# Way down of the feed-forward part by seven half-size products in place of eight, on one core of Trainium2

## The reference

```python
        gate, up = jnp.split(rmsnorm(x, g_ffn_pre[l]) @ w_ffn_in[l], 2, axis=-1)
        f = (jax.nn.silu(gate) * up) @ w_ffn_out[l]
        x = x + rmsnorm(f, g_ffn_post[l])
```

## Time and profile before

| | us |
|---|---|
| median of 3 runs | 1862.62 |
| lowest and highest | 1861.3 and 1863.35 |
| profiled execution, its own time | 1862.99 |
| its span, first to last instruction | 1861.2 |
| PE / DVE / ACT busy in the span | 1676.9 / 596.1 / 376.9 |
| mean granted clock of TensorE | 0.939 |

### The profile page before, as it was taken

How to read it: one execution, slowest core, us unless ns; L and a number is a source line. 1 busy time by engine, 2 the same in 40 slices (tenths; PEclk the granted TensorE clock), 3 DMA queues, 4 the chain that set the end, 5 groups by cost and what they waited for, 6 DMA issues and landing times.

```text
span 1861.2 us, 24768 instructions
## 1 busy us (share of the span) xinstructions
PE 1676.9 (90%) x10418; PEld 1070.4 (58%) x10418; DVE 596.1 (32%) x1235; ACT 376.9 (20%) x954; POOL 2.2 (0%) x6
## 2 busy tenths in 40 slices
PE   8999999999999999999999999999997766667666
PEld 5864758884477565688648768898863211102011
DVE  3482127550237422566106474232322000000001
ACT  4252122110224422211102561111202000000001
POOL 0000000000000000000000000000000000000000
PEclk9999999999999999999999999999998778767777
DMA  9313325444442242444453231211479999999997
GB/s 376 120 63 136 133 95 194 149 171 169 181 168 81 91 139 89 173 181 156 174 177 127 96 103 58 70 48 48 163 292 384 421 422 421 422 421 421 422 421 304
DMA packets 54089, 385.22 MB, mean 207 GB/s; under 512 B 6112, under 2 KB 6624, under 8 KB 8032
## 3 DMA queue, kind: packets, MB, share of 16 engines
q1 hardware_dynamic: 52272, 375.15, 51.5%
q10 hardware_dynamic: 1712, 8.52, 1.2%
HBM read 382.60 MB, written 1.05 MB: 206 GB/s over the span
## 4 chain that ended last, share of the span: by engine, by line
PE 70%; DMA 22%; DVE 4%; ACT 2%; issue 1%; SPq 0%; DVEq 0%; ACTq 0%
PE ps L177 50%; DMA arena<-in_stream 16%; DMA ring<-in_stream 5%; PE ps L1744 3%; PE ps L1725 2%; PE ps L1142 2%; PE ps L716 2%; DMA par<-in_stream 1%; PE ps L849 1%; PE ps L181 1%; DVE small L738 1%; PE ps L515 1%; PE ps L1885 1%; DVE arena L734 1%; PE ps L811 1%
## 5 line engine op out<-in xcount | busy, mean ns | idle before, releaser
L177 PE MATMUL ps<-arena 128*128 128x256 f32 (+2 forms) x2070 | 522.2, 550 | 86.3 <-DMA arena<-in_stream 80.8
L177 PEld LDWEIGHTS ps<-arena 128*128 128x128 f32 (+1 forms) x2070 | 271.4, 165 | 302.9 <-DMA arena<-in_stream 176.4
L177 PE MATMUL ps<-ring,arena 128*128 128x512 f32 (+4 forms) x1266 | 413.7, 569 | 33.9 <-DMA ring<-in_stream 29.6
L177 PEld LDWEIGHTS ps<-ring,arena 128*128 128x128 f32 (+1 forms) x1266 | 196.8, 176 | 228.1 <-issue 139.4
L177 PE MATMUL ps<-arena,ring 128*128 128x256 f32 x1260 | 302.2, 388 | 2.1 <-ACT arena L377 2.1
L177 PEld LDWEIGHTS ps<-arena,ring 128*128 128x128 f32 x1260 | 234.1, 191 | 46.9 <-issue 16.2
L2047 PE MATMUL ps<-arena 128*32 128x512 f32 x254 | 170.8, 779 | 0.0
L1097 DVE TENSOR_TENSOR arena<-ps,par 128x512 f32<-128x512 f32 x24 | 16.6, 690 | 263.6 <-ACT arena L1069 263.6
L2185 DVE TENSOR_TENSOR arena<-arena,ps 128x512 f32<-128x512 f32 x8 | 5.5, 687 | 259.4 <-PE ps L2047 259.4
L759 ACT ACTIVATE arena<-arena,small 128x256 f32<-128x256 f32 x112 | 55.7, 498 | 73.7 <-DVE small L746 73.7
L2047 PE MATMUL ps<-ring,arena 128*32 128x512 f32 x90 | 64.4, 823 | 0.0
(11 more groups left out here) (361 smaller groups left out, 1685.0 us busy)
## 6 DMA issues: line engine op xcount, KB each, us to landing
arena<-in_stream SPq DMA_DIRECT2D x175, 1024.0 KB, 26.3
ring<-in_stream SPq DMA_DIRECT2D x160, 1024.0 KB, 5.1
par<-in_stream SPq DMA_DIRECT2D x10, 1024.0 KB, 26.7
const<-in_stream SPq DMA_DIRECT2D x10, 1024.0 KB, 27.0
par<-in_layer_par ACTq DMA_DIRECT2D x3, 1664.0 KB, 8.9
const<-in_const SPq DMA_DIRECT2D x1, 1312.0 KB, 7.4
par<-in_layer_par ACTq DMA_DIRECT2D x2, 516.0 KB, 12.8
x<-in_x ACTq DMA_DIRECT2D x2, 512.0 KB, 7.0
```

The source lines that it names most:

```text
L177: ins = self.pe.e.matmul(out, lhsT, rhs, start=start, stop=stop)
```

## The change

The way down is split in two along each of its three sizes: tokens in blocks 0 and 1, hidden chunks in 0 to 10 ("first") and 11 to 21 ("second"), columns in halves. Each unit now holds chunk j and chunk 11 + j of the weights, as four quarters of 512 columns. Seven products of one block by one half, each with an accumulator of its own over the 11 units, take the place of eight: 1 to 7, on four banks of dve_tiles, two of both_tiles and one of act_tiles (product 1, which is not opened in the ring and waits for ACT's copy of group 9).

DVE makes sums of token blocks for four units at a time (down_tokens, four subtractions or additions up to 128 x 512) and of weights for each unit (down_sums: one subtraction 128 x 1024, which makes two sums, and two of 128 x 512). The sums of units 0 and 10 don't wait for a free buffer; the others wait until the unit two back has been given free. Those for unit 0 stand in the last group of gate and up, the rest behind its hidden rows.

In the last three units products 7 and 4 are left out and follow at the end, all three of 7 and then all three of 4; the three units are given free together behind them. DVE then adds the products to the four output tiles, in SBUF: block 0 from 1, 2, 6, 5 and 3, and its gain and residual; then 7 and block 1. ACT squares the tiles in SBUF, in the order (0,0), (1,0), (1,1), (0,1), and takes the next layer's columns of block 0 behind all four, where it took them ahead of the fourth. DVE takes its own columns of block 0 behind the gains of block 1, ahead of the addition to x.

```diff
+DOWN_ORDER = [(0, 0), (1, 0), (1, 1), (0, 1)]
+DOWN_HELD, DOWN_SUMS = FFN_GROUPS - 3, 4 * (FFN_GROUPS - 1)
...
+    pair = [first_mla + 4096 * i for i in (1, 0)]
+    p.down_both = [p.arena[:, at:at + 1024] for at in (pair[0], pair[1], pair[0] + 2048)]
+    p.down_sums = [[p.arena[:, at + 512 * i:at + 512 * i + 512] for i in range(4)] for at in (pair[0], pair[1], pair[0] + 2048)]
+    p.down_tokens = [[shaped(p.arena[:, at + 512 * i:at + 512 * i + 512], 4, P) for i in range(4)]
+                     for at in (pair[0] + 2048, pair[1] + 2048, first_pr)]
+    p.down_rows = shaped(p.arena[:, pair[1] + 2048:pair[1] + 4096], NB, D)
+    p.down_first, p.down_shared, p.down_middle = [p.arena[:, mark + 512 * i:mark + 512 * i + 512] for i in range(3)]
+    p.down_junk = p.arena[:, first_pr + 2048:first_pr + 3072]
...
+def down_residual_act(p, act, l, raw):
+    act.e.activation(p.small[:, 254:255], p.c("eps"), ACT.Sqrt).then_inc(act.step(), 1)
+    act.e.wait_ge(p.sem("down_first"), l + 1)
+    act.e.activation(p.down_first, p.mark["down_bank"], ACT.Copy).then_inc(
+        act.event("first_copied"), 1)
+    made = [(p.dve_tiles.drained, p.mark["down_dve"] - 3), (p.dve_tiles.drained, p.mark["down_dve"] - 1),
+            (p.both_tiles.drained, p.mark["down_both"] - 1), (p.both_tiles.drained, p.mark["down_both"])]
+    for t, (half, b) in enumerate(DOWN_ORDER):
+        act.e.wait_ge(*made[t])
+        act.e.activation(p.down_junk[:, 512 * (t % 2):512 * (t % 2) + 512], p.down_rows[:, b, half * 512:half * 512 + 512],
+                         ACT.Square, scale=D ** -0.5, accum_out=p.post_squares[:, t:t + 1]).then_inc(act.event("squared"), 1)
+        act.e.wait_ge(p.sem("squared"), 8 + t + 1)
+        base = p.post_squares[:, 4 + b:5 + b]
+        if t % 2 == 0:
+            act.e.activation(base, p.post_squares[:, t:t + 1], ACT.Identity, bias=p.c("eps")).then_inc(act.step(), 1)
+            act.e.wait_ge(act.steps, act.n)
+        else:
+            act.e.activation(p.post_root[:, b:b + 1], p.post_squares[:, t:t + 1], ACT.Sqrt, bias=base).then_inc(
+                act.event("post_root"), 1)
+    block_columns_act(p, act, *raw, 0)
...
+def down_residual_dve(p, dve, gain, raw):
+    first, u2, u4, u3 = p.down_first, p.down_shared, p.down_middle, p.down_first
+    def tile(half, b):
+        return p.down_rows[:, b, half * 512:half * 512 + 512]
+    def summed(out, left, ring):
+        dve.e.wait_ge(ring.full, ring.turn(dve))
+        dve.e.tensor_tensor(out, left, ring.take(dve), ALU.add).then_inc(ring.drained, 1)
+    def gained(half, b):
+        hs = slice(half * 512, half * 512 + 512)
+        dve.e.tensor_tensor(p.hrow[:, b, hs], tile(half, b), gain[:, hs], ALU.mult).then_inc(dve.step(), 1)
+    def added(b):
+        dve.e.wait_ge(dve.steps, dve.n)
+        dve.e.wait_ge(p.sem("post_root"), 4 + b + 1)
+        dve.e.reciprocal(p.rstd[:, b:b + 1], p.post_root[:, b:b + 1]).then_inc(dve.step(), 1)
+        dve.e.wait_ge(dve.steps, dve.n)
+        for half in range(2):
+            hs = slice(half * 512, half * 512 + 512)
+            dve.e.scalar_tensor_tensor(p.x[:, b, hs], p.hrow[:, b, hs], p.rstd[:, b:b + 1], p.x[:, b, hs],
+                                       ALU.mult, ALU.add).then_inc(dve.event("x_ready"), 1)
+    dve.e.wait_ge(p.sem("first_copied"), FFN_GROUPS)
+    summed(tile(0, 0), first, p.dve_tiles)
+    summed(u2, first, p.dve_tiles)
+    dve.e.wait_ge(p.dve_tiles.drained, p.dve_tiles.taken["dve"])
+    fifth = p.both_tiles.banks[p.both_tiles.taken["dve"] % p.both_tiles.size]
+    dve.e.wait_ge(p.both_tiles.full, p.both_tiles.turn(dve))
+    dve.e.tensor_tensor(u4, u2, fifth, ALU.add).then_inc(dve.step(), 1)
+    dve.e.wait_ge(dve.steps, dve.n)
+    summed(tile(1, 0), u4, p.dve_tiles)
+    gained(0, 0)
+    dve.e.wait_ge(p.dve_tiles.drained, p.dve_tiles.taken["dve"])
+    gained(1, 0)
+    added(0)
+    summed(u3, u2, p.dve_tiles)
+    dve.e.wait_ge(p.dve_tiles.drained, p.dve_tiles.taken["dve"])
+    summed(tile(1, 1), u3, p.both_tiles)
+    summed(tile(0, 1), u3, p.both_tiles)
+    dve.e.wait_ge(p.both_tiles.drained, p.both_tiles.taken["dve"])
+    gained(1, 1)
+    gained(0, 1)
+    block_columns_dve(p, dve, *raw, 0)
+    added(1)
...
-    def down(j):
-        u = w.next()
-        pe.e.wait_ge(p.act_tiles.drained, p.mark[f"turned{j}"])
-        for t, (half, b) in enumerate(BY_BLOCK):
-            if j == 0:
-                at = ring.index(acc[t])
-                pe.e.wait_ge(tiles.drained, max(n for n in range(tiles.opened) if n % tiles.size == at) + 1)
-            for c in range(2):
-                f = 2 * j + c
-                last = f == FC - 1
-                o = c * D + half * 512
-                ins = (pe.e.matmul if last else w.mm)(acc[t], p.h1T[:, f, b * P:(b + 1) * P],
-                                                      u[:, o:o + 512], start=f == 0, stop=last)
-                if last:
-                    ins.then_inc(p.dve_tiles.full, 1)
-        w.used()
...
+def down_pe(p, pe, w, tiles, ring, turn):
+    def last_use(bank):
+        at = ring.index(bank)
+        return max(n for n in range(tiles.opened) if n % tiles.size == at) + 1
+    p.mark["last_group"] = tiles.opened
+    acc = {1: p.act_tiles.banks[(p.act_tiles.opened + 1) % p.act_tiles.size]}
+    for name, of in ((2, p.dve_tiles), (6, p.dve_tiles), (3, p.dve_tiles), (7, p.dve_tiles), (5, p.both_tiles), (4, p.both_tiles)):
+        pe.e.wait_ge(of.drained, of.opened - of.size + 1)
+        acc[name] = of.open(pe)
+    p.mark["down_dve"], p.mark["down_both"], p.mark["down_bank"] = p.dve_tiles.opened, p.both_tiles.opened, acc[1]
+    signal = {1: p.sem("down_first"), 2: p.dve_tiles.full, 6: p.dve_tiles.full, 3: p.dve_tiles.full, 7: p.dve_tiles.full,
+              5: p.both_tiles.full, 4: p.both_tiles.full}
+    units = {}
+    def product(j, name):
+        if j == 0 and name == 1:
+            pe.e.wait_ge(p.act_tiles.drained, p.mark[f"turned{FFN_GROUPS - 2}"])
+        if j == 0 and name > 1:
+            pe.e.wait_ge(tiles.drained, last_use(acc[name]))
+        if name == 6:
+            pe.e.wait_ge(p.sem("token_sums"), 4 * (j // 4) + 8)
+            pe.e.wait_ge(p.sem("weight_sums"), DOWN_SUMS + 3 * j + 2)
+        if name == 4:
+            pe.e.wait_ge(p.sem("weight_sums"), DOWN_SUMS + 3 * j + 3)
+        b11, b12, b22, b21 = [units[j][:, 512 * i:512 * i + 512] for i in range(4)]
+        s1, s2, s3, s4 = [both[:, j % 4, :] for both in p.down_tokens[j // 4]]
+        t1, t3, t2, t4 = p.down_sums[down_buffer(j)]
+        first, second = p.h1T[:, j, :], p.h1T[:, FFN_GROUPS + j, :]
+        left, right = {1: (first[:, 0:P], b11), 2: (second[:, 0:P], b21), 3: (s4, b22), 4: (second[:, P:S], t4),
+                       5: (s1, t1), 6: (s2, t2), 7: (s3, t3)}[name]
+        last = j == FFN_GROUPS - 1
+        ins = (pe.e.matmul if last else w.mm)(acc[name], left, right, start=j == 0, stop=last)
+        if last:
+            ins.then_inc(signal[name], 1)
+        return ins
     for j in range(FFN_GROUPS):
-        down(j)
+        units[j] = w.next()
+        if j == FFN_GROUPS - 2:
+            pe.e.wait_ge(p.act_tiles.drained, p.mark[f"turned{FFN_GROUPS - 1}"])
+        for name in (2, 1, 6, 3, 7, 5, 4) if j == 0 else (1, 2, 6, 5, 3) if j >= DOWN_HELD else (1, 2, 6, 5, 3, 7, 4):
+            product(j, name)
+        if j < DOWN_HELD:
+            w.used()
         if j == 1:
             turn(FFN_GROUPS - 1)
+    for name in (7, 4):
+        for j in range(DOWN_HELD, FFN_GROUPS):
+            product(j, name)
+    w.used(FFN_GROUPS - DOWN_HELD)
+def down_buffer(j):
+    return 2 if j == FFN_GROUPS - 1 else j % 2
...
+    def down_tokens(batch):
+        rows = slice(4 * batch, min(4 * batch + 4, FFN_GROUPS))
+        rest = slice(FFN_GROUPS + rows.start, FFN_GROUPS + rows.stop)
+        n = rows.stop - rows.start
+        dve.e.wait_ge(p.act_tiles.drained, p.mark[f"turned{(rest.stop - 1) // 2}"])
+        a11, a21 = p.h1T[:, rows, 0:P], p.h1T[:, rows, P:S]
+        a12, a22 = p.h1T[:, rest, 0:P], p.h1T[:, rest, P:S]
+        s1, s2, s3, s4 = [both[:, 0:n, :] for both in p.down_tokens[batch]]
+        for i, (out, a, b, op) in enumerate(((s1, a21, a22, ALU.add), (s2, s1, a11, ALU.subtract),
+                                             (s3, a11, a21, ALU.subtract), (s4, a12, s2, ALU.subtract))):
+            if i in (1, 3):
+                dve.e.wait_ge(p.sem("token_sums"), 4 * batch + 4 + i)
+            dve.e.tensor_tensor(out, a, b, op).then_inc(dve.event("token_sums"), 1)
+    def down_sums(j):
+        v = p.mark["ffn_unit"] + 2 * FFN_GROUPS + j
+        if 2 <= j < FFN_GROUPS - 1:
+            dve.e.wait_ge(p.slots_free, p.units_freed + v - 1)
+        dve.e.wait_ge(p.slot_loaded[v % SLOTS], p.stream_base + 16 * (v // SLOTS + 1))
+        b11, b12, b22, b21 = [p.slots[v % SLOTS][:, 512 * i:512 * i + 512] for i in range(4)]
+        t1, t3, t2, t4 = p.down_sums[down_buffer(j)]
+        u = p.slots[v % SLOTS]
```

(38 more changed lines are left out.)

18 lines of the change are left out of this document (8 added, 10 removed).

## The result

The changed kernel took 1846.88 us in the median of four runs (1844.95 to 1848.66), the kernel before 1862.51 beside it: a ratio of 0.9916 with a 95% interval of 0.9904 to 0.9928, 15.6 us less. Forecast were 1848.0 in 1844.0 to 1852.0. The profiled execution took 1848.56 us, 14.4 less than the profiled one of before.

The account below looks back on a forecast made before the run. PE's matmul count was taken to bound the way down, weight transfers the last 361 us. Per layer 9.44 - 0.85 - 1.2 = 7.4 us, both 14.8, from 1862.99 to 1848.2 or 1847.8 from the median; given 1848.0, range 1844.0 to 1852.0.

Parts of the forecast that it names:

- The matmuls: Way down: 88 matmuls become 77 at 0.858 us each, 9.44 us less PE a layer; seven banks cost nothing.
- The sums: DVE beside the way down: about 37 us of sums a layer under 66 us of PE, never late, cost 0.
- The start: Start of the way down: product 1 waits for ACT's copy of group 9, cost 0.85 us a layer, bounds 0 and 1.6.
- The end: Behind the last product: ACT's columns stand behind all four squares, PE restarts 1.2 us later a layer, bounds 0 and 3.
- The slots: Last three units given free together, so five loads are issued late: cost 0; if uncovered, 5 us once.
- (d): Whole kernel: change doesn't do what it says, or a later transfer keeps its own time and meets the gain: 1862; chance 0.02.
- (a): Layer boundary: PE's clock falls behind the longer thin stretch; one fall gives 1851.4, two 1854.8; chance 0.15 for at least one.
- (b): Start and end of the way down: both waits hidden, ACT as early as before, 1844.1; chance 0.10.
- (c): Way down: DVE's sums set the pace, PE waits 2.6 us a unit, kernel slower at 1905; chance 0.03.

Follow-up runs that it names:

- fewer_products: Changed kernel with product 4 left out in eight of the eleven units, its sums still made, so the output is wrong; 1834.2 us, ratio 0.9850.
- sums_plus_one: Changed kernel with DVE making the 128 x 1024 subtraction of every unit twice; median 1848.3 us, stage unchanged at 70.76 us.
- start_with_6: Changed kernel with product 1 put behind products 2 and 6 in unit 0, not behind 2 alone; median 1847.92 us, stage 0.85 us shorter a layer.
- columns_before_last: Changed kernel with ACT taking the next layer's columns of block 0 ahead of the fourth square, not behind it; 1845.09 us.
- not_held: Changed kernel with products 7 and 4 of the last three units left in their units, not held to the end; median 1859.71 us, ratio 0.9988.
- start_and_columns: Changed kernel with the edits of start_with_6 and columns_before_last together; 1844.37 us, ratio 0.9904.
- turned_early: start_and_columns with PE's first-half transposes of block 0 ahead of the last product 4, and ACT's columns ahead of the third square; 1842.17 us, ratio 0.9895.
- idle_filled: not_held with matmuls of no use in PE's gaps: one ahead of block 0's transposes, three behind them; median 1852.84 us.
- sums_plus_four: Changed kernel with DVE making the 128 x 1024 sum of every unit five times; 1894.75 us, ratio 1.0181.

## Why the prediction was right, point by point

**The matmuls.** 11 x 0.858 = 9.44 us a layer stood in the sum. From the first record to E the stage lost 8.55. Product 1 starts 0.80 late (next point), and its two records take 0.96 from start to start of the next pair in place of 0.86; 8.55 + 0.80 + 0.10 = 9.45. fewer_products moved it by 8 matmuls more, to the hundredth. Seven banks in the place of four cost nothing.

**The sums: 0.** Right. DVE was busy for 38.5 us where near 40 were named. The walk through the first sums held in its rows, here the order of time of the changed kernel:

```profile
410.56 1.22 DVE L1475 TENSOR_TENSOR arena<-ring 128x1024 f32<-128x1024 f32 x1
...
412.54 0.69 DVE L1479 TENSOR_TENSOR arena<-ring,arena 128x512 f32<-128x512 f32 x1
...
414.08 0.42 DVE L1430 TENSOR_TENSOR arena<-arena,ps 128x256 f32<-128x256 f32 x1
...
416.32 0.69 DVE L1433 TENSOR_TENSOR arena<-arena,ps 128x512 f32<-128x512 f32 x1 [1.82 <-PE ps L1234]
```

The sums of unit 0 end at 413.23 (413.2 forecast), the first combining steps at 414.50 (414.8), though everything came 0.36 us later in this execution, and DVE then waits 1.82 us for PE, where 1.1 of room were forecast. sums_plus_one shows that the room elsewhere is over 1.3 us a unit.

**The start: 0.85.** 0.90 by the trace, 0.80 of wait (product 1 at 421.59 in place of 420.80) and 0.10 of the slower pair behind it, which I hadn't priced; start_with_6 gave back 0.85 of it.

**The end: 1.2.** 0.90. The path was the forecast one, ACT's columns behind the fourth square, and columns_before_last gave back exactly 0.90. What was too large is my count of hand-overs: DVE's additions and sums follow one another at their start with almost no gap, so tile (1,1) was ready at E - 0.02, not + 0.3, and the third square started at E + 0.02, not + 0.35; the fourth followed 1.08 later, and the columns came at E + 2.06 in place of + 2.35. The bound of 3 us was never near. Block 1's x was ready at E + 4.3 (4.6) and wanted at E + 6.2 (6.6). Block 0 was hidden, as forecast, and not_held prices what hides it: 3.4 us a layer, and by the clock 3.0 in the first and 1.4 in the second.

**The slots: 0.** Right. The two loads held back are issued at 487.75 and the other three from 488.93, and PE waits for no transfer there.

**The sum.** 7.4 us a layer forecast, 7.65 measured, 14.8 and 15.3; 15.0 of them are still there at the router's table (1408.5 to 1393.5) and 14.5 at the end of the span, so the transfer-bound rest began earlier by what the layers saved, within its own spread of 2 us. That was the ground on which rival (d) had been given 0.02. Of the 0.5 us by which the two layers gained more than forecast, the end gave 0.6 and the start took 0.1 back. The other 0.6 between 1848.0 and the median of 1846.88 lie inside the spread of the groups and have no cause here. One thing went well by luck: the sum took over the fall of the clock in the third block without naming it as a term. It was in both profiled executions, and it is worth 3.1 us where it is missing.

**The rivals.** (a), the clock behind the way down, didn't happen in the profiled executions of the changed kernel, but it is real: with the same restart at E + 3.33 one of the two boundaries of start_with_6 shows it, and with E + 6.75 both. Its cost in that one was 1.7 us, half of what I took from 1058. What I took was itself a little high: 6.8 us at the lower level cost 3.1 in the third block and 3.0 and 1.4 behind not_held's ways down, because PE is idle for a part of them. The like place that served as its price turned out to matter more than the boundary: it is there that executions of one kernel differ by 3 us. (b) fell, since both terms are there, but it was a fair bound: start_and_columns and turned_early, with other orders of the same instructions, come to 1844.4 and 1842.2. (c) fell for this kernel and was shown to exist, from a point more than 1.3 us of DVE a unit away. (d) fell: both ways down are 7.65 us shorter, and 14.5 of the 15.3 us are left at the end.

## What to carry to other kernels

A stage that is one unbroken chain of matmuls can be priced by their number to a few hundredths of a microsecond, and vector work beside it costs nothing as long as each piece is made one unit ahead (3.9 us of sums under 6.0 us of matmuls here); what has to be worked out are the two ends, the first wait and the order of the small operations behind the last product. There, ask of each engine what stands ahead of the one operation that TensorE waits for: moving that one forward by a place gave 0.9 us, and holding back products that nobody needs yet hid 3.4 us. A longer gap on TensorE can cost more than its length, because the clock may fall behind it: 4.4 us on top of 6.8 in not_held.

## What the runs showed of the hardware that was not expected

Products of no use in TensorE's gaps made a kernel faster: with the stages as long (74.18 us), not_held ran at 1.2 GHz behind each way down and idle_filled at a granted clock of 1.00, and that was worth 4.4 us by the traces and 4.7 by the medians within the groups. A fall of the same length doesn't always cost the same: 6.8 us at 1.2 GHz cost 3.0 us where PE had work for nearly all of them, and 1.4 where more than half had passed before PE restarted.

And a fall of the clock isn't a property of the program. The same place in the third block, with 1.5 us idle, shows 6.8 us at 1.2 GHz in two profiled executions of the changed kernel and none in the third; behind a way down the gap with 1.85 us idle was followed by a fall at one of fourteen boundaries in seven profiled executions (three of the changed kernel, one each of start_with_6, sums_plus_one, sums_plus_four and fewer_products), with 3.4 us at 1.2 GHz and 1.7 us lost. The Trainium skill, "TensorE: Matmul & The Clock Gate", section "Part 1: The HAM clock gate (the "warmup" mystery)", ties the half clock to idle time and says that the point at which one kernel gets back to the full clock varies from run to run. The traces here agree on the tie, by not_held and idle_filled; what varied here is whether the clock falls at all.
